# Attention scores in three fp32r passes, heads written out on two engines, and new places for gate loads and high rows

## The reference

```python
h = _rmsnorm(x, norm_w) * (1.0 + scale[:, None, :]) + shift[:, None, :]
proj = jnp.einsum("bsd,de->bse", h, w_in)
y_ssm = _ssd_branch(z_ssm, xbc, dt_raw, ...)
y_att = _fox_branch(q, k, v, z_att, f_logit, b_f)
merged = g_ssm * (y_ssm @ w_proj_ssm) + g_att * (y_att @ w_proj_att)
x = x + gate[:, None, :] * jnp.einsum("bsd,de->bse", merged, w_out)
```

```python
logits = jnp.einsum("bhqd,bhkd->bhqk", qi, k).astype(jnp.float32) * scale
logits = logits + fi[..., :, None] - f_cum[..., None, :]
logits = jnp.where(pi[:, None] >= kpos[None, :], logits, -jnp.inf)
probs = jax.nn.softmax(logits, axis=-1).astype(v.dtype)
return jnp.einsum("bhqk,bhkd->bhqd", probs, v)      # afterwards o * silu(z)
```

## Time and profile before

| | before |
|---|---|
| median of 3 runs | 1927.76 us (1924.55 to 1928.5) |
| the profiled execution | 1927.41 us, its span 1925.6 us |
| busy, share of the span | PE 97%, PEld 79%, DVE 61%, ACT 39%, POOL 9% |
| granted TensorE clock, mean | 0.997 |

### The profile page before, as it was taken

One profiled execution on the slowest core, in us unless ns is written; L12 is line 12 of the kernel. 1 busy time (PEld: TensorE's weight loads), 2 busy tenths in 40 slices (PEclk: granted clock), 3 DMA queues, 4 the chain that ended last, 5 costly groups with the idle time before them and its releaser, 6 DMA issues.

```text
span 1925.6 us, 26495 instructions
## 1 busy us (share of the span) xinstructions
PE 1875.6 (97%) x9556; PEld 1522.8 (79%) x9556; DVE 1178.6 (61%) x1541; ACT 750.7 (39%) x1146; POOL 169.7 (9%) x323
## 2 busy tenths in 40 slices
PE   7999999999999999999999999999999999999998
PEld 4787787787787887888888887878777878888786
DVE  6675544455457777767777444478344446766876
ACT  5424343335124535444444342342233335431423
POOL 1000110110000001000010000022100002110200
PEclk9999999999999999999999999999999999999999
DMA  9541665634332121221212843433301111211402
GB/s 362 143 77 36 115 101 114 110 121 146 138 110 55 56 55 44 76 77 55 55 56 90 292 156 93 131 121 94 107 23 47 35 33 44 66 34 31 140 31 99
DMA packets 169298, 181.21 MB, mean 94 GB/s; under 512 B 11010, under 2 KB 143546, under 8 KB 168314
## 3 DMA queue, kind: packets, MB, share of 16 engines
q1 hardware_dynamic: 155168, 130.69, 21.5%
q0 software_dynamic: 13760, 49.30, 11.7%
q10 hardware_dynamic: 282, 0.09, 0.0%
HBM read 139.56 MB, written 40.50 MB: 94 GB/s over the span
## 4 chain that ended last, share of the span: by engine, by line
PE 81%; DVE 6%; DMA 4%; ACT 3%; issue 2%; PEld 1%; DVEq 1%; SPq 1%; ACTq 1%; PEldq 0%; POOL 0%; POOLq 0%
PE acc L285 22%; PE acc L304 21%; PE acc L1609 15%; PE work L1617 3%; PE acc L1634 3%; PE acc L3127 3%; PE acc L2586 2%; PE work L1626 2%; PE work L2567 1%; PE acc L1023 1%; PEld acc L285 1%; PE work L2576 1%; PE acc L3434 1%; DMA dskip<-in_d_skip 1%; DVE conv_out L847 1%
## 5 line engine op out<-in xcount | busy, mean ns | idle before, releaser
L304 PE MATMUL acc<-ha_hi,w_hi 128*128 128x512 f32 x640 | 258.1, 403 | 3.5 <-DVE nxt L2383 1.6
L304 PE MATMUL acc<-ha_hi,w_lo 128*128 128x512 f32 x640 | 250.4, 391 | 0.0
L304 PE MATMUL acc<-ha_lo,w_hi 128*128 128x512 f32 x640 | 249.7, 390 | 0.0
L285 PE MATMUL acc<-ha_hi,w_hi 128*128 128x512 f32 x592 | 185.9, 395 | 6.6 <-ACT ha_hi L564 1.9
L285 PE MATMUL acc<-ha_lo,w_hi 128*128 128x512 f32 x592 | 183.9, 392 | 1.6 <-DVE ha_lo L725 1.6
L285 PE MATMUL acc<-ha_hi,w_lo 128*128 128x512 f32 x592 | 183.0, 390 | 0.0
L261 ACT ACTIVATE w_hi<-w_raw 128x1024 fp32r<-128x1024 f32 x96 | 101.2, 1054 | 180.4 <-PE acc L304 80.8
L265 DVE TENSOR_TENSOR w_lo<-w_raw,w_hi 128x1024 fp32r<-128x1024 f32 x96 | 117.6, 1225 | 50.4 <-ACT w_hi L261 47.9
L304 PEld LDWEIGHTS acc<-ha_hi,w_hi 128*128 128x128 f32 x640 | 120.6, 188 | 28.4 <-issue 4.5
L304 PEld LDWEIGHTS acc<-ha_hi,w_lo 128*128 128x128 f32 x640 | 120.1, 188 | 26.2
L304 PEld LDWEIGHTS acc<-ha_lo,w_hi 128*128 128x128 f32 x640 | 120.6, 188 | 22.6
(11 more groups left out here) (517 smaller groups left out, 3610.6 us busy)
## 6 DMA issues: line engine op xcount, KB each, us to landing
w_raw<-in_w_in SPq DMA_DIRECT2D x99, 512.0 KB, 4.1
acs_bc<-acs_scr POOLq DMA_DIRECT2D x8, 1024.0 KB, 16.0
w_raw<-in_w_out SPq DMA_DIRECT2D x11, 512.0 KB, 3.9
x_tok<-in_x SPq DMA_DIRECT2D x8, 512.0 KB, 7.3
w_scale<-in_w_ada SPq DMA_DIRECT2D x8, 512.0 KB, 9.7
w_shift<-in_w_ada SPq DMA_DIRECT2D x8, 512.0 KB, 8.9
xt_scr<-xt SPq DMA_DIRECT2D x1, 4096.0 KB, 13.3
w_ada_g<-in_w_ada SPq DMA_DIRECT2D x8, 512.0 KB, 13.4
```

The lines of the kernel that those rows point to most:

```text
L285: mm = pe.matmul(acc[:, n % 2, h * HALF:(h + 1) * HALF], w[:, n % 2, k, :], x[:, k, h * HALF:(h + 1) * HALF], start=(k == 0 and i == 0), s ...
L304: mm = pe.matmul(acc[:, 0, half * HALF:(half + 1) * HALF], w[:, n % 2, k, :], x[:, k, half * HALF:(half + 1) * HALF], start=(k == 0 and i ...
```

## The change

Scores: GpSimd splits q and k into `q_hi`, `k_hi` (copies to fp32r) and `q_lo`, `k_lo` (subtractions), and `scores(t)` makes three fp32r passes for each chunk, at least 256 columns wide. Block 4 is cut 0:3, 3:5 instead of 0:4, 4:5, and the others as before. To make room, y's gated halves are written over `silu_za`, and y's high and low halves over `prob_t` and `silu_za`, so each half is stored before its place is used again. Products 12 and 13 move on TensorE, y's halves are split one by one, v's copy comes at the end of the head before, and gate(1) and others change places. `t4`'s split moves into head 0. ScalarE and VectorE have their eight heads written out. Stage 3: one `split_lo` earlier. Stage 4: GpSimd's loop is written out, with each gate load ahead of the save. Stages 11 and 12: the four high rows lie where the last fill does not read, so ScalarE makes them during it; VectorE makes the low rows 0 to 3 ahead of the stage's start; TensorE starts stage 12 without `begin_stage`. Counts of semaphores follow. The core of the diff:

```diff
@@ stage 3, VectorE
-                if f in (4, 6):
-                    split_lo(dve, N_GATT + (2 if f == 4 else 3))
+                if f == 6:
+                    split_lo(dve, N_GATT + 3)
                 if f + 1 < KT:
                     gated(f + 1)
+                if f == 3:
+                    split_lo(dve, N_GATT + 2)
                 low(f)
@@ stage 4, GpSimd
+            for i in range(KT):
+                b = i % 2
+                if i < 2:
+                    pool.dma_start(gate4[:, b, :], g_scr[:, i, :]).then_inc(g_loaded4[b], 16)
+                else:
+                    pool.wait_ge(mix4_done, i + 1)
+                    pool.dma_start(gate4[:, b, :], g_scr[:, i, :]).then_inc(g_loaded4[b], 16)
+                    save_mix(pool, i - 2)
@@ stage 5, places and chunks
+        y_lo_1st = Region(at_gated, arena_end)("y_lo_1st", [P, HALF], F32R)
+        y_split = Region(at_split, arena_end)
+        y_hi_half = y_split("y_hi_half", [P, HALF], F32R)
+        y_lo_2nd = y_split("y_lo_2nd", [P, HALF], F32R)
...
+            cuts = [0, t + 1] if t < BANK_TILES else [0, min(BANK_TILES, t - 1), t + 1]
@@ stage 5, GpSimd
-                pool.tensor_copy(q_t[:, :], next_tiles[0][:, :])
-                pool.tensor_copy(k_t[:, :], next_tiles[1][:, :])
+                pool.tensor_copy(q_hi[:, :], next_tiles[0][:, :])
+                pool.tensor_copy(k_hi[:, :], next_tiles[1][:, :])
+                pool.drain()
+                pool.tensor_tensor(q_lo[:, :], next_tiles[0][:, :], q_hi[:, :].bitcast(F32), ALU.subtract)
+                pool.tensor_tensor(k_lo[:, :], next_tiles[1][:, :], k_hi[:, :].bitcast(F32), ALU.subtract)
                 pool.drain().then_inc(taken, 1)
@@ stage 5, TensorE
-                        pe.matmul(work[:, c % 2, 0:(b - a) * P], q_t[:, t * P:(t + 1) * P], k_t[:, a * P:b * P],
-                                  start=True, stop=True).then_inc(qk_done, 1)
+                        w = max(b - a, 2) * P
+                        for i, (q, k) in enumerate(((q_hi, k_hi), (q_hi, k_lo), (q_lo, k_hi))):
+                            mm = pe.matmul(work[:, c % 2, 0:w], q[:, t * P:(t + 1) * P], k[:, a * P:a * P + w],
+                                           start=(i == 0), stop=(i == 2))
+                        mm.then_inc(qk_done, 1)
...
-                for t in range(5, NT):
+                for t in range(5, NT - 1):
                     turn_probs(t)
                     fill(t + 5)
                     weigh_values(t)
+                fill(12)
+                turn_probs(NT - 1)
                 fill(13)
+                weigh_values(NT - 1)
@@ stage 5, ScalarE
+                if h == 0:
+                    take_values(0)
                 act.wait_ge(pair_added, 10 * h + 10)
+                act.wait_ge(x_lo_done, LO_SPLITS[5] + 2 * h if h else T_BASE + 3)
                 act.activation(silu_za[:, :], next_tiles[3][:, :], ACT.Silu)
...
+                if h == 0:
+                    t_hi(4, t4_hi, quad_21[:, :, :])
                 act.wait_ge(x_lo_done, T_BASE + 4)
+                act.wait_ge(y_saved, Y_SAVED + 64 * h)
                 copies(0)
...
+                    act.wait_ge(y_gated, 2 * h + 3)
+                    act.wait_ge(pv_done, NT * h + 7)
+                    act.activation(y_hi_half[:, :], silu_za[:, T1], ACT.Copy).then_inc(x_hi_done, 1)
                     hi(14)
                     hi(15)
                     hi(16)
+                    take_values(h + 1)
+                    act.wait_ge(y_gated, 2 * h + 4)
+                    act.wait_ge(y_saved, Y_SAVED + 32 + 64 * h)
+                    act.activation(y_hi_half[:, :], silu_za[:, T2], ACT.Copy).then_inc(x_hi_done, 1)
...
-            with act.Fori(0, FOX_HEADS // 2 - 1) as j:
-                head(2 * j, 0)
-                head(2 * j + 1, 1)
+            for h in range(FOX_HEADS):
+                head(h, h % 2, last=(h == FOX_HEADS - 1))
@@ stage 5, VectorE (its heads are written out in the same way)
+                def y_low(half, dst):
+                    dve.wait_ge(x_hi_done, SPLITS[5] + 2 * h + half + 1)
+                    dve.tensor_tensor(dst[:, :], silu_za[:, half * HALF:(half + 1) * HALF], y_hi_half[:, :].bitcast(F32),
+                                      ALU.subtract).then_inc(x_lo_done, 1)
...
                 gate(0)
                 add_kept5(1)
+                if not last:
+                    y_low(0, y_lo_1st)
                 read(12)
...
                     weight_sums(dve, 2, h)
                     lo(14)
+                    lo(15)
+                read(13)
                 gate(1)
                 if not last:
-                    lo(15)
+                    lo(16)
+                    y_low(1, y_lo_2nd)
                     weight_sums_in_place(dve)
@@ stages 11 and 12
+                if p == PAIRS - 1:
+                    low_row(dve, 0)
                 read_next(7)
...
-            begin_stage(pe, 12)
             pe.wait_ge(nxt_ready, NXT_READY)
...
+            pe.wait_ge(ml_gated, PAIRS + 1)
             first_partial()
...
+            act.wait_ge(rows_read11, ROWS_READ11)
+            act.wait_ge(ml_gated, PAIRS)
+            for k in range(4):
+                act.activation(y2_hi[k], y2[:, k, :], ACT.Copy).then_inc(x_hi_done, 1)
             begin_stage(act, 12)
...
+            for k in range(1, 4):
+                low_row(dve, k)
             begin_stage(dve, 12)
```

More of the change, by code:

```diff
@@ L1364, in pool_4 @@
             pool.wait_ge(ga_saved, 16 * (KT + 1))
[L1365 to L1373, removed]
+            for i in range(KT):
[6 more added lines that the diff above has]
+                    save_mix(pool, i - 2)
+            for i in range(KT - 2, KT):
+                pool.wait_ge(mix4_done, i + 3)
+                save_mix(pool, i)
             end_stage(pool, 4)
         ar = arena()
-        q_t = ar("q_t", [P, T])
-        k_t = ar("k_t", [P, T])
+        q_hi = ar("q_hi", [P, T], F32R)
+        k_hi = ar("k_hi", [P, T], F32R)
+        q_lo = ar("q_lo", [P, T], F32R)
         v_tok = ar("v_tok", [P, NT, FOX_D])
+        at_gated = ar.at
         silu_za = ar("silu_za", [P, T])
@@ L1439, in fox_chunks @@
             first = sum((v + BANK_TILES) // BANK_TILES for v in range(t))
-            return [(first + i, a, min(a + BANK_TILES, t + 1)) for i, a in enumerate(range(0, t + 1, BANK_TILES))]
+            cuts = [0, t + 1] if t < BANK_TILES else [0, min(BANK_TILES, t - 1), t + 1]
+            return [(first + i, a, b) for i, (a, b) in enumerate(zip(cuts, cuts[1:]))]
         FC = fox_chunks(NT)[0][0]
@@ L1531, in save_y @@
             def save_y(h):
-                wait_here(sp, x_lo_done, LO_SPLITS[5] + h + 1)
-                for i in range(2):
-                    sp.dma_start(row(y_hi_scr, h)[:, i * HALF:(i + 1) * HALF], y_hi[i][:, :].bitcast(F32)).then_inc(y_saved, 16)
-                sp.dma_start(row(y_lo_scr, h), y_lo[:, :].bitcast(F32)).then_inc(y_saved, 16)
+                for i, lo in enumerate((y_lo_1st, y_lo_2nd)):
+                    s = slice(i * HALF, (i + 1) * HALF)
+                    wait_here(sp, x_lo_done, LO_SPLITS[5] + 2 * h + i + 1)
+                    sp.dma_start(row(y_hi_scr, h)[:, s], y_hi_half[:, :].bitcast(F32)).then_inc(y_saved, 16)
+                    sp.dma_start(row(y_lo_scr, h)[:, s], lo[:, :].bitcast(F32)).then_inc(y_saved, 16)
             load_pair((Q_OFF + P, K_OFF + P), 0, 0)
@@ L1724, in act_5, with take_values @@
             first_hi(2)
-            t_hi(4, t4_hi, quad_21[:, :, :])
+            def take_values(h):
+                act.wait_ge(v_turned, h + 1)
+                act.activation(v_tok[:, :, :], work[:, 2:4, :], ACT.Copy).then_inc(v_ready, 1)
             def head(h, odd, last=False):
@@ L1918, in head @@
                 lo(6)
+                if h == 0:
+                    t_lo(4, t4_lo, quad_21[:, :, :], t4_hi)
                 normalise(1)
@@ L1958, in head @@
                     lo(14)
+                    lo(15)
+                read(13)
                 gate(1)
                 if not last:
[L1961 removed]
+                    lo(16)
+                    y_low(1, y_lo_2nd)
                     weight_sums_in_place(dve)
[L1963 to L1964 removed]
                 if last:
+                    dve.wait_ge(x_hi_done, SPLITS[5] + 2 * h + 2)
                     dve.wait_ge(late_saved[0], LATE_SAVED)
[L1967 to L1980 removed]
+                    dve.tensor_tensor(ya_lo[:, FOX_HEADS - 1, :], silu_za[:, :], ya_hi[:, FOX_HEADS - 1, :].bitcast(F32), ALU.subtract
+                                      ).then_inc(x_lo_done, 2)
+            for h in range(FOX_HEADS):
+                head(h, h % 2, last=(h == FOX_HEADS - 1))
             end_stage(dve, 5)
@@ L2775, in fill @@
                 def fill(q):
-                    project_part(pe, N_ML + 4 * (p + 1) + q // 4, q % 4, FILLS10 + 4 * p + q // 4)
+                    last = p == PAIRS - 1 and q == 14
```

(6 more changed lines are left out.)

85 lines of the change are left out of this document (31 added, 54 removed).

## The result

The kernel after takes 1910.16 us (median of four runs, 1908.1 to 1910.63) against 1928.13 beside it (1924.55 to 1928.63): a ratio of 0.9907 [0.9894, 0.9919], 18.0 us less, and by the interval of the ratio between 15.6 and 20.4. The forecast was 1909.5. Its profiled execution took 1908.1 us, with a span of 1906.2.

The account below looks back on a forecast made before the run. TensorE, busy 97% of the span, was taken as the bound. Terms 10.2 + 2.35 - 1.4 + 0.4 + 0.3 + 3.7 + 2.3 = 17.9 us off 1927.41 gave 1909.5 us, range 1903 to 1919.

Parts of the forecast that it names:

- three-pass scores: Scores in eight heads: three fp32r passes instead of plain fp32 save 1.28 us a head, 10.2 us (bounds 3 to 13).
- heads written out: Starts of loop iterations on ScalarE and VectorE: straight code removes branch stalls in the last two, saving 2.35 us.
- new order at the head's end: Chain from turn(7) to fill(2), and fill(7): cover used up, 0.2 us charged in seven heads, cost 1.4 us.
- head 0: First head: wait for keep(0) goes, fill(7) waits about 1.5 us; net gain 0.4 us (bounds -2 and 1.9).
- stage 3: TensorE starts a product after a 0.41 us gap behind its w_lo; the earlier split saves 0.3 us.
- stage 4: Earlier gate loads remove TensorE's 2.02 us wait and the 1.7 us lost at low clock: 3.7 us saved.
- stages 11 and 12: Earlier high and low rows save 2.3 us (bounds 0 and 4.8); idle at partial(1) and the slow stretch stay.
- rival of unhidden weight loads: Scores: narrow fp32r passes do not hide their weight loads, so they save 3, not 10.2 us: 1916.7; chance 0.09.
- sign that I gave against part 1: Scores: if narrow fp32r passes start over 0.15 us apart, the estimate of the scores' saving is wrong.
- Small waits should appear: Heads: fill(2) should wait on the kept copy and fill(7) on w_lo, each under 0.3 us.
- slower rival: fill(2) in seven heads: chain 2 us longer, each head idles and falls to low clock, 26 us lost: 1934; chance 0.04.
- The port: Heads: GpSimd's two subtractions, 1.91 us each, hold up VectorE by up to 3.8 us through the shared port; taken as hidden.

Follow-up runs that it names:

- one-product kernel: The kernel after with scores as one plain fp32 product again, same chunks, GpSimd's subtractions gone: 1918.35 us, ratio 0.9964.
- heads written out alone: The kernel before with only the heads of ScalarE and VectorE written out, nothing else: 1922.1 us, ratio 0.9987.
- stage 12 back: The kernel after with the high and low rows of stages 11 and 12 back in their old places: 1910.76 us, ratio 0.9923.
- twice the silu: The kernel after with ScalarE's silu of 1.06 us done twice in each head, a drain between: 1915.9 us, ratio 0.9955.

## Why the prediction was right

The medians moved by 18.0 us, the forecast was 17.9. That they meet to 0.1 is luck: the measured gain is known to some 2.4 us either way, and the kernel before took 1925.36, 1925.93 and 1924.8 beside the experiments for 1928.13 here. Most mechanisms held; term by term, the gain of the two profiled executions is 1.4 us larger than the forecast's, which is just what I had charged to the new order in vain, and the other misses cancel. In microseconds of the profiled executions:

| term | forecast | measured | from |
|---|---|---|---|
| three-pass scores | -10.2 | -9.6 | one-product kernel, 8 x 1.20 |
| heads written out | -2.35 | -2.35, and -1.5 in head 0 | heads written out alone |
| new order at the head's end | +1.4 | 0 | heads of 59.06 and 59.07 |
| head 0 | -0.4 | -0.2 in all | 60.97 to 59.55, less 1.2 of scores |
| stage 3 | -0.3 | -0.7 | 474.57 for 475.26; the gap is gone in each profile with the moved split, and in the two others with the old place it is 0.33 and 0.43 |
| stage 4 | -3.7 | -3.9 (-4.2 alone) | 4.6 ahead at its end (553.03 for 557.61), less stage 3; 1.7 of it is the low clock, and 2.1 is the gain against a kernel without it |
| stages 11 and 12 | -2.3 | -3.2; -1.4 by the order | 16.7 to 19.9 ahead; stage 12 back |

- **Scores.** The narrow passes were as estimated, 0.17 to 0.18 and 0.12; the first pass behind plain fp32 matmuls costs 0.08 more (0.20 at 772.45 for 0.12), which I had not counted, and the 1.28 a head became 1.20; how much of the difference it makes up wasn't counted. The rival of unhidden weight loads is out for 384 and 256 columns. The sign that I gave against part 1, narrow passes over 0.15 apart, was ill put: my own 0.175 for 384 columns lies above it, and it can only be read for 256.
- **The branch** was right in size and place. I missed its share in head 0 and credited t4's move with it. That move by itself cost: written out alone, head 0 takes 59.48; with the scores' 1.2 off it should be 58.3 in the kernel after, and it is 59.55. The wait there is the one of fill(5) for keep(3), 1.43, behind t_hi(4) and the wait for t_lo(4), not fill(7)'s for lo(7) as I wrote. Gain and cost cancelled nearly as forecast.
- **The head's end** is the step that failed. I charged 0.2 a head because I took a counted margin of zero for a cost. The chain measured 12.7, not 13.0, so the slack is 0.3. "Small waits should appear" did not come true. The direction was right: twice the silu costs 0.95 a head, and the slower rival with its place, its condition and its 1934 came out at 1933.5 once the chain was made some 2.1 us longer (the wait of 1.82 and the slack of 0.3). What I had wrong there is that each head would fall to the low clock, where three of seven did in the profile, and that no gap below its length reaches it; that 26 was counted and 23.8 came makes the match of the two times partly luck.
- **The port.** Two subtractions took 2.6 and 2.8 us instead of 1.91, and VectorE's two steps took 4.1 us longer, not up to 3.8, of which only 2.4 delayed it. So normalise(7) ended 1.7 us before turn(7), where I had 1. The idle time that took up the rest was missing from my count. That the new order is the cover, and the price without it, 8.4 us, the prediction named only in half a sentence; it should have been a rival of its own.
- **The clock.** I took the low clock in stages 4 and 12 as fixed to the idle time ahead of it. It was gone in stage 12 in the profile of the kernel after, where I kept it, and the one in stage 4 came in one of two profiles with the old stage 4 there (before, not in the kernel with written-out heads alone), so its 1.7 us are no sure gain. That gaps at or under 1.7 leave the clock full held in the kernel before and not in later kernels: it fell once behind 1.53, and once behind 1.66 and 1.05. Why it comes behind one idle stretch of 1.8 or 2.8 us and not behind the next of the same length stays open.

The measured terms, head 0 taken whole, sum to 20.0 us; 0.5 is given back between stage 4 and head 0, where scores(0) waits 0.33 for `taken`, and 0.5 at the end of the span, against 0.2 won at stage 6: 19.2, for 19.3 measured. That the medians differ by less, 18.0, fits a low clock that comes in some executions: the three other executions of the kernel after, at 1910.16 to 1910.63, have a mean granted clock of 0.995 or 0.996, the profiled one at 1908.1 has 0.997, and 0.001 of the span is 1.9 us.

## What to carry to other kernels

When one part of a change puts load on an engine that shares something with another, ask which step of the queue is then late and whether another edit of the same change moves its reader; test the two together and apart. A margin of zero in a count is no cost, it is a place to measure: one added operation of known length shows the slack at once. Price idle time of TensorE of 1 to 3 us with and without the low clock behind it, and take the mean, not the one case that a single profile happens to show.

## What the runs showed of the hardware

- A wait of TensorE costs more than the list of waits says: heads grew by 0.95 us for a listed 0.71, by 1.18 for 0.94 to 1.02, and by 2.08 for 1.82, about 0.25 each time. At 722.90, with the silu twice, 0.17 of it is in the count: the idle time starts at the modelled end of the last matmul (0.34 long), while its successor would have started 0.17 behind its start. Another 0.10 is in the first matmul behind the wait, whose successor starts 0.33 behind it for 0.23.
- An fp32r pass takes about the time of its columns down to 256 (0.228, 0.175, 0.12 us at 512, 384 and 256) and hardly less at 128 (0.11 to 0.14), so padding a 128-column chunk to 256 costs next to nothing (0.07 us for three passes), and cutting 640 columns as 384 + 256 is 0.11 us cheaper than 512 + 128.
- VectorE's multiplication of 1024 columns by a column of one value takes 0.75 us alone and 2.63 beside a GpSimd subtraction, which itself takes 2.6 and 2.8, for the 1.91 of the one in stage 12, which began ahead of VectorE's. Beside GpSimd's conversions a pair of VectorE's subtractions took 1.92 where 1.29 is usual.
- Idle stretches of TensorE of 1.8 to 2.1 us were followed by 3.4 us at 1.2 GHz in three of seven cases, and those of 2.8 us by 3.4 us or more in three of eight, with the same instructions around them. Shorter ones are not safe: it came once behind 1.53, and once behind 1.66 and 1.05, where most profiles with 1.4 to 1.7 us of idle time kept the full clock.
